# The largest routed expert moved ahead of the first pair of small experts in a two-layer denoising step

## The chip, the core and the metric

The kernel is one program on one core of a Trainium2 chip. The core has TensorE (PE in the profile, with its weight loads as PEld), VectorE (DVE), ScalarE (ACT), GpSimd (POOL) and SyncE (SP), which here issues nearly all transfers from HBM. The metric is the device time of one execution in microseconds (us); lower is better. The profile is one execution of its own.

## What is computed

The reference is a two-layer step over 128 context tokens and 128 latent tokens of width 1024, all in float32. Each layer has a mixer (attention in layer 0, a gated DeltaNet in layer 1) and then a mixture of 16 SwiGLU experts of inner width 512. Only the mixture matters here:

```python
in_group = (jnp.arange(N_EXPERTS) // EXPERTS_PER_GROUP)[None, :] == group_sel[:, None]
_, idx = lax.top_k(jnp.where(in_group, biased, -jnp.inf), TOP_K)
...
for e in range(N_EXPERTS):
    he = jax.nn.silu(x @ wg[e]) * (x @ wu[e])
    y = y + gates[:, e:e + 1] * (he @ wd[e])
```

Each of the 256 tokens goes to 2 of the 16 experts. The weights of an expert are three pieces of 2 MB: two halves of gate and up together (m = 0 and 1, each half of the contraction), and the down matrix (m = 2). So a layer reads 48 pieces of 2048 KB.

## The kernel before

**The ring.** All big weights of the program stream through `ring`, six slots of 2048 KB in SBUF, in one fixed order of positions. SyncE walks through that order: for each position it waits until the slot is free (`slot_free`, L1886) and issues one transfer (L1887). In a layer's expert stage the 48 positions are listed by `SEQ` (L43). In this text T0 to T47 are those 48 transfers. T(n) goes into the slot that T(n-6) held, so it can be issued when the last use of T(n-6) is over.

**Ranks and units.** Experts 4 and 5 of the model always come first, as ranks 0 and 1 (the fixed pair). The other 14 are sorted by their token count on the chip; rank 2 is the largest, rank 15 the smallest. `UNITS` (L42) gives the order in which ranks are worked on. A unit of two ranks is a pair: two experts with at most 32 tokens each, which share one block of 64 tokens. A unit of one rank is an expert with a block of 64 tokens of its own, or, for ranks 2, 3 and 4, two blocks of 64 one after the other on the same weights (`LEAN_CAP`, 128 tokens). `LEAN` lists the 14 blocks of a layer. (`FULL` is a second branch for token counts that do not fit; the profiled execution takes `LEAN`.) Within a pair `SEQ` alternates the two ranks: m = 0 of both, m = 1 of both, m = 2 of both.

**A block on TensorE.** `products` (gate and up, L544), `combined` of the block before (L570), two pairs of transposes (L475 and L587), then `down` (L562). Between them ScalarE and VectorE make SiLU(gate) * up, and GpSimd has gathered the block's tokens ahead of it (L885). The slots are given back by the last block that uses them: m = 0 in the middle of `products` by TensorE itself (L547), m = 1 after `products`, when ScalarE has read the result (L650), m = 2 after `down` (L658):

```python
for r in freed(plan, n):
    act.sem_inc(slot_free[slot_of(n0, r, m)], 1)
```

`freed(plan, n)` (L450) names the ranks that no later block uses. So the first of the two blocks of rank 2, 3 or 4 gives back nothing, and the second gives back three slots.

**The start of a stage.** T0 to T5, the fixed pair, are loaded before the stage starts. The fixed pair's `products` run ahead of the routing's end; ScalarE then gives back four slots at once (T6 to T9 are issued), and its `down`, much later, the other two (T10 and T11).

Of the kernel before, what the change touches and what calls it, by code (L numbers as in the profile page):

```python
# [38 lines left out]

FIXED = (4, 5)  # L40
FIXED_CAP, FIXED_SLOTS = 32, 64
UNITS = ((0, 1), (8, 9), (2,), (5,), (10, 11), (3,), (6,), (12, 13), (4,), (7,), (14, 15))  # L42
SEQ = [(r, m) for unit in UNITS for m in range(3) for r in unit]  # L43
LEAN_CAP = (FIXED_CAP,) * 2 + (128,) * 3 + (64,) * 3 + (32,) * 8


def full_cap(r):

    return T if r < 2 else min(T, 2 * T // (r - 1))


LEAN = [b for unit in UNITS for b in ([tuple((r, 0) for r in unit)] if len(unit) == 2 else
                                      [((unit[0], 64 * j),) for j in range(LEAN_CAP[unit[0]] // 64)])]
FULL = LEAN[:1] + [((r, at),) for unit in UNITS for r in unit for at in range(FIXED_CAP if r < 2 else 0, full_cap(r), 64)]
SLOTS_PAD = 3 * T
# [1977 lines left out]
```

## Time and profile before

| what | value |
|---|---|
| median of 3 runs | 1121.9 us (1112.18 to 1123.24) |
| profiled execution, its own time | 1118.37 us |
| its span, first to last instruction | 1116.4 us |
| PE busy | 980.3 us (88% of the span) |
| ring<-slots transfers | 138 of 2048 KB each |
| DMA over the span | 268 GB/s on average |
| granted TensorE clock, mean | 0.934 |

Of the page's 40 slices, those from about 280 us to 515 us and from about 880 us to 1088 us are the two expert stages; there the line with GB/s shows 424 to 430 in most slices. PE's share of the span is an average over stages that have different limits, and a slow or waiting PE can look busy. Times inside a stage are given in us from the span's start.

### The profile page before, as it was taken

To read this page: it belongs to the slowest core of one execution; us is meant where nothing else is said; L and a number is where in the kernel's file an instruction comes from. 1 tells how busy PE (TensorE), PEld (TensorE's weight loads), DVE (VectorE), ACT (ScalarE), POOL (GpSimd) and SP (SyncE) were. 2 spreads that over 40 slices of the span, in tenths; PEclk is the share of its full clock that TensorE was granted. 3 is DMA by queue.
4 is the path that set the end of the run, shared out by engine and by line. 5 is a ranking of instruction groups with operands and counts; after the bars stand their busy time and mean duration, and the time that the engine had idled before them with its cause. 6 is when DMAs were issued, how large, how long until landed. Compare 5 with 4: busy or idle time off the path is not lost. (4 is left out here: it accounts for less than half of the span.)

```text
span 1116.4 us, 13823 instructions
## 1 busy us (share of the span) xinstructions
PE 980.3 (88%) x5476; PEld 568.5 (51%) x5476; DVE 346.9 (31%) x816; ACT 216.9 (19%) x513; POOL 134.5 (12%) x149
## 2 busy tenths in 40 slices
PE   4799999797889898987999999888696989898996
PEld 1344456675333342336787668678584423333334
DVE  0100115238201000024333676668516400101014
ACT  1211045112200010003233421213103210000013
POOL 1000000001000000001000166566001000000000
PEclk8699998896989999998999899989897889999999
DMA  9985782053899999996564500222225499999991
GB/s 382 424 354 217 291 333 93 1 213 166 331 430 428 424 429 428 426 427 293 198 254 161 216 2 1 76 76 76 76 83 219 189 415 427 427 429 426 429 420 42
DMA packets 22444, 299.50 MB, mean 268 GB/s; under 512 B 2592, under 2 KB 2720, under 8 KB 4320
## 3 DMA queue, kind: packets, MB, share of 16 engines
q1 hardware_dynamic: 20880, 292.45, 64.0%
q0 software_dynamic: 1488, 6.03, 1.4%
q8 instruction: 49, 0.80, 0.3%
q14 instruction: 27, 0.22, 0.1%
HBM read 295.32 MB, written 3.15 MB: 267 GB/s over the span
## 5 line engine op out<-in xcount | busy, mean ns | idle before, releaser
L544 PE MATMUL bank<-ring,arena 128*32 128x512 f32 (+1 forms) x1216 | 203.6, 610 | 6.5 <-DMA ring<-slots 6.5
L562 PE MATMUL bank<-ring,arena 128*32 128x512 f32 (+1 forms) x608 | 111.7, 665 | 30.9 <-DMA ring<-slots 25.8
L544 PEld LDWEIGHTS bank<-ring,arena 128*32 128x32 f32 (+1 forms) x1216 | 61.3, 125 | 144.3 <-issue 133.6
L818 DVE TENSOR_TENSOR arena<-arena,bank 128x256 f32<-128x256 f32 x28 | 11.8, 421 | 301.5 <-ACT arena L647 301.5
L972 PE MATMUL bank<-act_t,ring 128*128 128x256 f32 x384 | 89.2, 386 | 6.3 <-DVE act_t L429 6.3
L1533 PE MATMUL bank<-ring,act_t 128*128 128x512 f32 x192 | 88.2, 615 | 3.9 <-ACTq L279 3.9
L972 PEld LDWEIGHTS bank<-act_t,ring 128*128 128x128 f32 x384 | 72.2, 193 | 20.0 <-DVE act_t L429 6.7
L562 PEld LDWEIGHTS bank<-ring,arena 128*32 128x32 f32 (+1 forms) x608 | 31.5, 133 | 92.6 <-issue 82.7
L307 PE MATMUL bank<-ring,par 128*32 128x512 f32 x384 | 54.6, 693 | 15.2 <-DMA ring<-slots 14.0
L885 POOL COPY arena<-arena 128x512 f32 (+1 forms) x34 | 17.5, 515 | 393.1 <-PE bank L544 306.7
L902 PE MATMUL bank<-act_t,ring 128*128 128x256 f32 x256 | 61.2, 402 | 1.6 <-ACT act_t L1264 0.9
L1533 PEld LDWEIGHTS bank<-ring,act_t 128*128 128x128 f32 x192 | 36.7, 196 | 50.7 <-issue 46.8
L570 PE MATMUL bank<-arena 64*128 64x256 f32 x448 | 55.9, 389 | 1.7 <-ACTq L467 1.7
L902 PEld LDWEIGHTS bank<-act_t,ring 128*128 128x128 f32 x256 | 51.9, 204 | 10.3 <-ACT act_t L1264 1.2
L570 PEld LDWEIGHTS bank<-arena 64*128 64x128 f32 x448 | 41.0, 186 | 28.6 <-issue 21.3
L647 ACT ACTIVATE arena<-bank 128x256 f32<-128x256 f32 x28 | 10.7, 383 | 180.2 <-PE bank L544 180.2
L659 ACT ACTIVATE arena<-bank 128x512 f32<-128x512 f32 x28 | 16.7, 597 | 141.3 <-PE bank L562 141.3
L441 POOL TENSOR_SCALAR res<-res,small 128x256 f32<-128x256 f32 x24 | 12.9, 550 | 239.9 <-DVE act_t L429 239.9
L326 DVE TENSOR_TENSOR mod<-bank,par 128x8 f32<-128x8 f32 x24 | 3.8, 161 | 115.0 <-PE bank L319 115.0
L319 PEld LDWEIGHTS bank<-par,o_delta 128*128 128x128 f32 x192 | 26.5, 212 | 15.8 <-ACT o_delta L313 11.7
L822 DVE COPY arena<-bank 128x256 f32<-128x256 f32 x28 | 11.9, 425 | 67.1 <-PE bank L587 67.1
L307 PEld LDWEIGHTS bank<-ring,par 128*32 128x32 f32 x384 | 11.3, 119 | 40.3 <-issue 39.5
(320 smaller groups left out, 1290.4 us busy)
## 6 DMA issues: line engine op xcount, KB each, us to landing
ring<-slots SPq DMA_DIRECT2D x138, 2048.0 KB, 12.5
cst<-consts SPq DMA_DIRECT2D x1, 1260.5 KB, 31.8
act_t<-x_t POOLq DMA_DIRECT2D x1, 1024.0 KB, 12.4
ring<-state POOLq DMA_DIRECT2D x1, 1024.0 KB, 7.7
out_st<-arena POOLq DMA_DIRECT2D x4, 256.0 KB, 2.8
out_y<-arena SPq DMA_DIRECT2D x4, 256.0 KB, 2.1
par<-params SPq DMA_DIRECT2D x1, 613.0 KB, 4.0
arena<-nat_bias POOLq DMA_DIRECT2D x1, 512.0 KB, 20.2
```

The source lines that it names most:

```text
L307: last = pe.matmul(bk[32 * j:32 * j + 32, :], p_("cond")[:, 32 * c:32 * c + 32], w[:, c, :], start=(c < 4), stop=(c >= 4))
L319: last = pe.matmul(bk[:, 2 * m:2 * m + 2], ada_rowbuf[:, job % 2, m * P:(m + 1) * P], p_("fold")[:, 0:2], start=True, stop=True)
L441: pool.tensor_scalar(res[:, c, :], res[:, c, :], ln_scaled[:, 0 + i:i + 1], ln_scaled[:, 64 + i:65 + i], ALU.mult, ALU.add).then_inc(S("re ...
L544: last = pe.matmul(bk[to:to + wide, :], x[:, 4 * m + c, wide * e:wide * e + wide], w[:, c, 512 * t:512 * t + 512], start=(m == 0 and c == ...
L562: last = pe.matmul(bank[3][to:to + wide, :], ht[:, col + wide * e:col + wide * e + wide], w[:, f, 512 * t:512 * t + 512], start=(f == 0), ...
L570: last = pe.matmul(bank[4 + d // 2][:, (d % 2) * T:(d % 2) * T + T], yb[64 * t:64 * t + 64, b, o * P:(o + 1) * P], gb[64 * t:64 * t + 64, ...
L659: act.activation(yb[:, n % 2, :], bank[3][:, :], ACT.Copy).then_inc(S("y_copied"), 1)
L822: dve.tensor_copy(gb[:, n % 2, :], bank[n % 2][:, 0:256]).then_inc(S("gates_moved"), 1)
L885: last = pool.tensor_copy(xe[:, n % 2, :, wide * e:wide * e + wide], xg[:, :, bass.ds(at + j, wide)])
L902: last = pe.matmul(out_bank(q, b, o), w[:, c, m * P:(m + 1) * P], act_t[:, c, :], start=(c == 0), stop=(c == KC - 1))
L972: last = pe.matmul(bank[i % 3][:, 0:T], w[:, c, (i % 4) * P:(i % 4 + 1) * P], act_t[:, c, :], start=(c == 0), stop=(c == KC - 1))
L1533: last = pe.matmul(bank[n % 4][:, :], act_t[:, c, s * P:(s + 1) * P], w[:, c, :], start=(c == 0), stop=(c == KC - 1))
```

## The change

```diff
-UNITS = ((0, 1), (8, 9), (2,), (5,), (10, 11), (3,), (6,), (12, 13), (4,), (7,), (14, 15))
+UNITS = ((0, 1), (2,), (8, 9), (5,), (10, 11), (3,), (6,), (12, 13), (4,), (7,), (14, 15))
 SEQ = [(r, m) for unit in UNITS for m in range(3) for r in unit]
```

Rank 2, with its two blocks, now stands directly behind the fixed pair, and the pair of ranks 8 and 9 behind it. `SEQ`, `LEAN` and `FULL` follow from the table, and so the order of transfers, of TensorE's blocks and of the gathers, in both layers. SyncE's instructions are the same as before, wait for wait; only the weights that a transfer fetches differ. T6 to T11 were ranks 8 and 9 and T12 to T14 were rank 2; now T6 to T8 are rank 2 and T9 to T14 are ranks 8 and 9.

On TensorE, in the LEAN branch of layer 0, directly behind the fixed pair's `down` (64x512 is a block of one expert, 32x512 that of a pair), there stood before:

```order
L544 MATMUL bank<-ring,arena 32x512 x32
L570 MATMUL bank<-arena 128x256 x8
L475 MATMUL bank<-cst,arena 128x128 x2
L587 MATMUL bank<-cst,arena 128x128 x2
L562 MATMUL bank<-ring,arena 32x512 x16
L544 MATMUL bank<-ring,arena 64x512 x16
```

In the same place there stands now:

```order
L544 MATMUL bank<-ring,arena 64x512 x16
L570 MATMUL bank<-arena 128x256 x8
L475 MATMUL bank<-cst,arena 128x128 x2
L587 MATMUL bank<-cst,arena 128x128 x2
L562 MATMUL bank<-ring,arena 64x512 x8
L544 MATMUL bank<-ring,arena 64x512 x16
```

The pair's block is gone from there, and the two blocks of rank 2 follow each other. On TensorE two blocks further on, directly ahead of rank 5, there stood before the second block of rank 2:

```order
L544 MATMUL bank<-ring,arena 64x512 x16
L570 MATMUL bank<-arena 128x256 x8
L475 MATMUL bank<-cst,arena 128x128 x2
L587 MATMUL bank<-cst,arena 128x128 x2
L562 MATMUL bank<-ring,arena 64x512 x8
L544 MATMUL bank<-ring,arena 64x512 x16
```

And now the pair of ranks 8 and 9:

```order
L544 MATMUL bank<-ring,arena 32x512 x32
L570 MATMUL bank<-arena 128x256 x8
L475 MATMUL bank<-cst,arena 128x128 x2
L587 MATMUL bank<-cst,arena 128x128 x2
L562 MATMUL bank<-ring,arena 32x512 x16
L544 MATMUL bank<-ring,arena 64x512 x16
```

The last row of each is rank 5, which stands where it stood. Layer 1 changes in the same way.

## Rows read from the trace of the kernel before

**Rows 1.** Busy time by stretch, inside both expert stages.

```profile
core 0: us, PE busy (x) PEld busy (x) DVE busy (x) ACT busy (x) POOL busy (x), PEclk, DMA share, GB/s
315.00:320.00 5.00, 3.01 (x16) 0.91 (x20) 0.00 (x0) 0.00 (x0) 0.00 (x0) 0.50 1.02 434
...
310.00:515.00 205.00, 177.63 (x1060) 72.37 (x1060) 28.99 (x80) 24.61 (x53) 7.32 (x14) 0.97 1.01 428
907.00:1085.00 178.00, 163.64 (x962) 62.43 (x960) 17.43 (x54) 16.08 (x37) 7.16 (x14) 0.96 1.01 428
```

**Rows 2.** TensorE's timeline, layer 0: start, us, line, count, [idle before, releaser].

```profile
302.95 7.05 PE L544 MATMUL bank<-ring,arena 128*32 128x512 f32 x64
...
316.99 5.71 PE L562 MATMUL bank<-ring,arena 128*32 128x512 f32 x32 [4.48 <-DMA ring<-slots]
...
326.69 3.65 PE L544 MATMUL bank<-ring,arena 128*64 128x512 f32 x16 [0.41 <-DMA ring<-slots]
...
336.60 7.04 PE L544 MATMUL bank<-ring,arena 128*64 128x512 f32 x32
...
349.89 7.04 PE L544 MATMUL bank<-ring,arena 128*64 128x512 f32 x32
...
493.66 3.64 PE L562 MATMUL bank<-ring,arena 128*32 128x512 f32 x32 [2.88 <-DMA ring<-slots]
```

**Rows 3.** TensorE's waits in layer 0, one releaser: us in total, times, longest.

```profile
PE bank L562 <- DMA ring<-slots: 13.5, 4, 4.5
```

**Rows 4.** L1887, layer 0, one transfer at a time: issue (T10, T18, T47), landing.

```profile
L1887 SPq DMA_DIRECT2D ring<-slots x1: 338/338/338, 303.4 to 303.4; - x1
...
DMA to landing us min/median/max: 7.9/7.9/7.9
...
L1887 SPq DMA_DIRECT2D ring<-slots x1: 338/338/338, 340.4 to 340.4; - x1
...
DMA to landing us min/median/max: 11.2/11.2/11.2
...
L1887 SPq DMA_DIRECT2D ring<-slots x1: 338/338/338, 481.5 to 481.5; - x1
...
DMA to landing us min/median/max: 12.0/12.0/12.0
```

**Rows 5.** SyncE's issues in layer 0: start, us (T12, T19, T20).

```profile
306.76 0.34 SPq L1887 DMA_DIRECT2D ring<-slots  x1
...
343.88 0.34 SPq L1887 DMA_DIRECT2D ring<-slots  x1
...
350.30 0.34 SPq L1887 DMA_DIRECT2D ring<-slots  x1
```

**Rows 6.** A transfer issued alone, long before the stage (L1887).

```profile
L1887 SPq DMA_DIRECT2D ring<-slots x1: 328/328/328, 177.9 to 177.9; - x1
...
DMA to landing us min/median/max: 7.5/7.5/7.5
```

**Rows 7.** Layer 1: transfers T10 and T18, issue and landing (L1887).

```profile
L1887 SPq DMA_DIRECT2D ring<-slots x1: 338/338/338, 899.9 to 899.9; - x1
...
DMA to landing us min/median/max: 7.8/7.8/7.8
...
L1887 SPq DMA_DIRECT2D ring<-slots x1: 338/338/338, 937.4 to 937.4; - x1
...
DMA to landing us min/median/max: 10.8/10.8/10.8
```

**Rows 8.** TensorE's timeline, layer 1.

```profile
899.47 7.17 PE L544 MATMUL bank<-ring,arena 128*32 128x512 f32 x64
...
912.79 6.47 PE L562 MATMUL bank<-ring,arena 128*32 128x512 f32 x32 [3.63 <-DMA ring<-slots]
...
923.73 3.65 PE L544 MATMUL bank<-ring,arena 128*64 128x512 f32 x16 [0.89 <-DMA ring<-slots]
...
1090.25 3.64 PE L562 MATMUL bank<-ring,arena 128*32 128x512 f32 x32 [2.83 <-DMA ring<-slots]
```

## The prediction

> **What bounds the kernel now.** First the page's slices, to find the two expert stages, since the change touches nothing else. Then the busy time by stretch inside them: in both the DMA engines are busy throughout (share 1.01 in each long stretch) at 428 GB/s [rows 1]. TensorE is busy for 177.63 of 205 us in the first, so it looks nearly as loaded; but the waits say who waits for whom. In layer 0 TensorE waits for weights in `down` four times, 13.5 us in all [rows 3], once for each pair behind the fixed one, the last time in front of the very last piece (at 493.66 [rows 2]); nothing in the stretch shows the transfers short of free slots for long enough to stop. So the stage ends when its 48th piece has landed, plus one `down`; what TensorE does earlier decides only when slots come free.
>
> The pace of the stream: T18 is issued at 340.4 and lands 11.2 us later, at 351.6; T47 is issued at 481.5 and lands at 493.5 [rows 4]. 29 pieces in 141.9 us is **4.89 us a piece**. Layer 1 runs alike: T18 lands at 937.4 + 10.8 = 948.2 [rows 7], the last wait ends at 1090.25 [rows 8], 4.90 us a piece. A unit's price on TensorE is about the same for every block, 13.29 us from one block's start to the next (336.60 to 349.89 [rows 2]), but its price in pieces is not: a pair takes 6 pieces, 29.3 us of stream, a one-block expert 14.7 us, and rank 2, 3 or 4 takes 14.7 us of stream for 26.6 us of TensorE, and holds its slots through most of them.
>
> **The change part by part.** No instruction is added or removed. GpSimd makes one gather less ahead of the first block behind the fixed pair and one more two blocks later; TensorE comes to these blocks 13 us apart, which hides a gather, and VectorE's and ScalarE's work only changes places. Their cost is nothing, and if the cover were gone it would be one gather. SyncE's queue has the same waits in the same order, so what counts is when each wait is met. I follow the slots through layer 0.
>
> T6 to T9 are issued when the fixed pair's `products` are over, T10 and T11 when its `down` is over (303.4 [rows 4]); neither depends on who comes next. T10 lands at 311.3, T11 4.89 us later at 316.2.
>
> Before, the block behind the fixed pair was ranks 8 and 9, started at 302.95 [rows 2]. It uses its slots once, so 3.81 us after its start SyncE could already issue T12 (306.76 [rows 5]), five more followed, and the stream never ran dry.
>
> Now rank 2 starts there at the same 302.95 (its pieces are T6 to T8; the pair in this place began on T6 to T9 and did not wait). Its first block gives back nothing. The second starts 13.29 us later, at 316.24. From rank 2's second block before, which started at 336.60 [rows 2], the offsets of its releases can be read: T18 was issued 3.80 [rows 4], T19 7.28 and T20 13.70 us after it [rows 5]. So now **T12 is issued at 320.04, T13 at 323.5, T14 at 329.9**. At 320.04 nothing is left in flight, since T11 landed at 316.2. How long a piece takes into an empty stream is bounded by the nearest rows: 7.5 us [rows 6] for one issued quite alone, 7.9 and 7.8 us for T10 [rows 4, 7], which others follow closely. T12 here is alone for 3.5 us; I take the middle, 7.75, so it lands at 327.8. Without the hole it would have landed at 316.2 + 4.89 = 321.1; the hole is 6.7 us.
>
> Behind T12 the stream holds. T13 could land at 331.3 by its issue and at 332.7 by the pace, so the pace decides; T14 comes out level (337.7 by issue, 337.6 by pace). Ranks 8 and 9 start at 316.24 + 13.29 = 329.5 and give back their first halves 3.81 us later, so T15 and T16 are issued from 333.3 on, ahead of the 334.8 at which T15 is due at that lead of 7.75 us (342.5 by pace); T17 and T18 follow on the second halves, about 337 to 338. So T18 lands at 327.8 + 6 x 4.89 = 357.1, against 351.6 before: **5.5 us late**. Before was not at the ideal pace in this stretch: from T10 at 311.3 to T18 at 351.6 it took 40.3 us for 8 pieces, 5.04 each. If the six pieces behind the hole run at that, T18 lands at 358.0, 6.4 us late. I take 5.9, since the irregular pieces before lay among issues in quick succession and half of that remains.
>
> The Trainium skill has a fit for one transfer ("DMA: Bandwidth & Descriptors", section Anatomy of one DMA: about 2.0 us and the bytes at 436 GB/s), made on another issuing path than SyncE's. By it a lone piece of 2.1 MB would take an estimated 6.8 us and the sum would be 1.9 us smaller over both layers; the rows show 7.5 and more, so the rows are used.
>
> Layer 1 has the same steps: 899.47 [rows 8] + 13.29 + 3.80 = 916.56 for T12, landing at 924.3, and T18 at 953.7, against 948.2: 5.5 us late; at the pace that stretch had (907.7 to 948.2, 8 pieces, 5.06 each) it is 6.5. I take 5.9 again.
>
> Is the delay kept? From T18 on the order of units is the old one. TensorE is now short of weights: rank 5 starts at 329.5 + 13.3 = 342.8, waits a little for T16 (347.4) and is done near 357; the pair 10, 11 waits for T19 (362.0), T21 (371.8) and T23 (381.6) and is over 3.6 us behind the last, at 385, or at 389 if that `down` runs at half the clock. Rank 3's first block starts behind T24 (386.5) or at 389, its second 13.3 us later, at 400 to 402, and releases T30 at 404 to 406, which could land at 413.7 at the latest and is due by pace at 357.1 + 12 x 4.89 = 415.8. So there is no second hole, with 2 us to spare, and from there on the old picture comes back, shifted. The next stage's weights go into slots that the last pair gives back, so they shift too, and the work between the two expert stages hangs on the first one's end. What TensorE no longer waits for in ranks 8, 9 and 2 (4.48 and 0.41 us in layer 0 [rows 2]) it waits for later, in ranks 5, 10 and 11.
>
> The sum is 5.9 + 5.9 = 11.8 us (10.9 to 12.9 by the bounds). On the profiled execution's 1118.37 us (span 1116.4) that is 1130.2 us; on the median of the runs shown, 3.5 us above it, 1133.7. I take **1133 us**, about 1% more.
>
> **The rivals.** *TensorE's lost time comes back.* The change puts 26.6 us of TensorE's work over 14.7 us of stream just where TensorE stood still for weights. If TensorE set the stage's end, layer 0 would gain the 4.48 and 0.41 us of waiting and the 2.07 us by which the `down` behind the wait ran long (5.71 against 3.64 [rows 2]; the granted clock there is 0.50, the lower of its two levels, behind the 4.48 us of idle time [rows 1]), and layer 1 3.63 + 0.89 + 2.83 [rows 8]: 14.3 us, 1104 us on the profile and 1107.6 on the median. For it speaks that PE is busy in 87% of the stretch; against it that every later pair waits for its last piece again [rows 3] and the last one up to the end.
>
> This rival is what the Trainium skill would make one expect: "Perfetto Trace Analysis", section Optimization Strategies under DMA, sets as the goal to keep the matmul engine as highly used as possible. The stretch's own rows contradict it here, since the stream is full and TensorE's use can rise only by taking slots from it.
>
> *Only one of the two holes counts.* If the work between the stages were waiting for something that does not hang on the first stage, or if pieces behind a hole came faster than 4.89 us, one hole's 5.9 us would vanish: 1124.3 on the profile, 1127.8 on the median, no change within what can be told. The rows show the stream at a steady 428 GB/s with all engines busy, so it cannot catch up inside a stage; the chain between stages I have no row against.
>
> *A second hole at rank 3.* The pair 10, 11 now waits three times for 3.6 to 6.3 us. After 4.48 us of waiting the trace shows a `down` that begins at the lower clock. If more of the pair's halves and of rank 3's first block run so, at 3.5 us more for each, the 2 us to spare are gone and up to 3.5 us a layer come on top: 1137 on the profile, 1140.7 on the median. It decides when rank 3's second block starts later than 404 in the changed trace's layer 0.
>
> **How the numbers follow.** Forecast 0.76, one hole only 0.10, TensorE's time 0.05, second hole 0.09. About 1% is what a measurement of this kernel can tell from no change, here 11.2 us, just under the forecast's 11.8; so of the forecast's 0.76 I put 0.50 above the line and 0.26 inside it. That gives slower 0.59, same 0.36, faster 0.05. The range: the forecast by its bounds is 1129 to 1135, the runs before lay up to 10 us below their median and 1.3 above, and it should take in part of the two nearest rivals: 1123 to 1139. It leaves out the fast rival and the far ends of the other two, about 0.15.
>
> **What would show it.** In the changed trace T12 is issued 16.6 us behind T10 instead of 3.4, and lands 11 to 12 us behind T11; the DMA share drops below 1 for some 6 us near 316 to 322 and near 913 to 919 and nowhere else in the stages; ranks 8 and 9 run without a wait; the pair 10, 11 waits at both halves; the last `down` of layer 0 waits until about 499.5, that of layer 1 until about 1102. If T12 is issued at 306, or the stream still runs dry nowhere, the forecast is wrong; if layer 0 ends 6 us late and layer 1's start is not, the second rival is right.

## The result and the profile after

Four runs of the changed kernel have a median of 1136.15 us (1132.28 to 1141.19); before, on the same occasion, 1122.57 us (1112.18 to 1123.87). The ratio is 1.0158, 95% interval 1.0119 to 1.0197: **slower by 1.6%**. The 1133 us on record are inside what was measured, but stand for a change of 1.0%, on the border of what can be told; the size was too small. On the 1121.9 us that the forecast started from, the measured ratio gives 1139.6 us, 0.6 us above the upper end of its range.

The profiled execution after is the longest of the four: 1141.19 us, span 1139.3, against 1118.37 and 1116.4. So its 22.9 us over before must first be divided. I cut each span at T6's issue and T47's landing of both stages:

| piece of the span | before | after | difference |
|---|---|---|---|
| up to T6's issue, layer 0 | 281.9 | 287.7 | 5.8 |
| stage of layer 0 (T6's issue to T47's landing) | 211.6 | 220.1 | 8.5 |
| from there to T6's issue, layer 1 | 385.6 | 387.1 | 1.5 |
| stage of layer 1 | 211.0 | 218.2 | 7.2 |
| the rest | 26.3 | 26.2 | -0.1 |

15.6 us lie in the two stages. Whether the 5.8 us ahead of them belong to the change is a question for the experiments.

The busy time by stretch after, layer 0, in the form of [rows 1]:

```profile
310.00:320.00 10.00, 9.74 (x56) 4.10 (x52) 1.36 (x4) 0.77 (x2) 0.80 (x2) 1.00 0.96 395
320.00:327.00 7.00, 7.00 (x34) 2.31 (x32) 0.00 (x0) 0.60 (x1) 0.00 (x0) 1.00 0.17 43
327.00:515.00 188.00, 162.72 (x996) 62.71 (x994) 17.30 (x54) 16.36 (x36) 6.70 (x13) 0.95 1.00 424
```

There is the hole: 7 us in which the DMA engines move 43 GB/s instead of 428, while TensorE is busy for all 7.00 of them at full clock. Single transfers of layer 0 after (L1887; T10, T12 and T14, each issue with its time to landing) answer to [rows 4]:

```profile
L1887 SPq DMA_DIRECT2D ring<-slots x1: 337/337/337, 308.8 to 308.8; - x1
...
DMA to landing us min/median/max: 7.7/7.7/7.7
...
L1887 SPq DMA_DIRECT2D ring<-slots x1: 342/342/342, 325.7 to 325.7; - x1
...
DMA to landing us min/median/max: 8.5/8.5/8.5
...
L1887 SPq DMA_DIRECT2D ring<-slots x1: 338/338/338, 335.6 to 335.6; - x1
...
DMA to landing us min/median/max: 9.4/9.4/9.4
```

T12 is issued nearly 17 us behind T10 (before 3.4), and T14 nearly 27 us behind it. TensorE's timeline of the same stretch, in the form of [rows 2]:

```profile
308.51 7.09 PE L544 MATMUL bank<-ring,arena 128*64 128x512 f32 x32
...
321.85 7.04 PE L544 MATMUL bank<-ring,arena 128*64 128x512 f32 x32
...
335.24 7.07 PE L544 MATMUL bank<-ring,arena 128*32 128x512 f32 x64
...
345.12 3.64 PE L562 MATMUL bank<-ring,arena 128*32 128x512 f32 x32 [0.29 <-ACT arena L655]
350.00 3.65 PE L544 MATMUL bank<-ring,arena 128*64 128x512 f32 x16 [1.24 <-DMA ring<-slots]
354.80 3.66 PE L544 MATMUL bank<-ring,arena 128*64 128x512 f32 x16 [1.15 <-DMA ring<-slots]
...
369.58 6.05 PE L544 MATMUL bank<-ring,arena 128*32 128x512 f32 x32 [4.70 <-DMA ring<-slots]
379.50 6.21 PE L544 MATMUL bank<-ring,arena 128*32 128x512 f32 x32 [3.87 <-DMA ring<-slots]
...
408.89 7.04 PE L544 MATMUL bank<-ring,arena 128*64 128x512 f32 x32
...
507.90 5.16 PE L562 MATMUL bank<-ring,arena 128*32 128x512 f32 x32 [3.34 <-DMA ring<-slots]
```

Rank 2's two blocks start at 308.51 and 321.85, 13.34 us apart, and ranks 8 and 9 at 335.24 run through without waiting for weights (345.12 waits only for ScalarE). The waits come back at rank 5, 1.24 and 1.15 us, and at the pair 10, 11, 4.70 and 3.87 us in front of its two halves. TensorE's waits for weights in layer 0, from the fixed pair's `down` to the end of the stage, sum to 22.1 us now:

```profile
PE bank L544 <- DMA ring<-slots: 14.2, 7, 4.7
PE bank L562 <- DMA ring<-slots: 7.9, 3, 3.5
```

Before, they summed to 17.3 us, the 13.5 us in `down` [rows 3] and these in `products`:

```profile
PE bank L544 <- DMA ring<-slots: 3.8, 4, 1.3
```

In `down` they fell from 13.5 us to 7.9, and in `products` they rose from 3.8 to 14.2. A reader who looked only at the first number would think the change had worked.

### The profile page after: what moved, and what is told of

The parts are those of the page before. It is cut to its first block and busy times, and to the rows that moved or that the text cites. A ratio compares the mean times of both kernels' runs of the same rounds, so it can differ in the third digit from the quotient of the medians.

```text
span 1139.3 us, 13823 instructions
## 1 busy us (share of the span) xinstructions
PE 991.2 (87%) x5476; PEld 573.9 (50%) x5476; DVE 347.1 (30%) x816; ACT 216.8 (19%) x513; POOL 134.4 (12%) x149
## 5 line engine op out<-in xcount | busy, mean ns | idle before, releaser
L544 PE MATMUL bank<-ring,arena 128*32 128x512 f32 (+1 forms) x1216 | 211.8, 639 | 27.6 <-DMA ring<-slots 27.6
L562 PE MATMUL bank<-ring,arena 128*32 128x512 f32 (+1 forms) x608 | 108.3, 641 | 21.7 <-DMA ring<-slots 16.0
L818 DVE TENSOR_TENSOR arena<-arena,bank 128x256 f32<-128x256 f32 x28 | 11.8, 421 | 317.0 <-ACT arena L647 317.0
L972 PEld LDWEIGHTS bank<-act_t,ring 128*128 128x128 f32 x384 | 72.2, 193 | 19.9 <-DVE act_t L429 6.7
L307 PE MATMUL bank<-ring,par 128*32 128x512 f32 x384 | 55.5, 703 | 15.7 <-DMA ring<-slots 14.6
L902 PEld LDWEIGHTS bank<-act_t,ring 128*128 128x128 f32 x256 | 51.6, 202 | 10.1 <-ACT act_t L1264 1.2
L647 ACT ACTIVATE arena<-bank 128x256 f32<-128x256 f32 x28 | 10.7, 383 | 210.4 <-PE bank L544 210.4
```

The lines of the kernel that those rows point to most:

```text
L307: last = pe.matmul(bk[32 * j:32 * j + 32, :], p_("cond")[:, 32 * c:32 * c + 32], w[:, c, :], start=(c < 4), stop=(c >= 4))
L544: last = pe.matmul(bk[to:to + wide, :], x[:, 4 * m + c, wide * e:wide * e + wide], w[:, c, 512 * t:512 * t + 512], start=(m == 0 and c == ...
L562: last = pe.matmul(bank[3][to:to + wide, :], ht[:, col + wide * e:col + wide * e + wide], w[:, f, 512 * t:512 * t + 512], start=(f == 0), ...
L902: last = pe.matmul(out_bank(q, b, o), w[:, c, m * P:(m + 1) * P], act_t[:, c, :], start=(c == 0), stop=(c == KC - 1))
L972: last = pe.matmul(bank[i % 3][:, 0:T], w[:, c, (i % 4) * P:(i % 4 + 1) * P], act_t[:, c, :], start=(c == 0), stop=(c == KC - 1))
```

## The experiments

The theory, from here on the hole theory: a stage is as long as its stream of 48 pieces; rank 2 holds three of six slots through two blocks, and with rank 2 first there is nothing else to give back, so the stream stands still once in every stage. The rivals: a loss outside the stages; a loss from the order of the pieces itself; TensorE's time deciding; and, within the theory, which slot sets the hole. The table has the stage lengths of each run's profiled execution (T6's issue to T47's landing, us) and the ratio to before of the timed runs. Edits of `UNITS` are shown against the kernel before, the others against the changed kernel; before_early_down and after_early_down are one edit on either.

| kernel | layer 0 | layer 1 | ratio, 95% interval |
|---|---|---|---|
| before | 211.6 | 211.0 | |
| after | 220.1 | 218.2 | 1.0158 (1.0119 to 1.0197) |
| only_l0: new order in layer 0 alone | 219.6 | 212.3 | 1.0086 (1.0053 to 1.0119) |
| only_l1: new order in layer 1 alone | 212.6 | 219.0 | 1.0073 (1.0038 to 1.0108) |
| one_block_first: rank 5 in rank 2's place | 211.5 | 211.3 | 0.9982 (0.9941 to 1.0022) |
| two_doubles: ranks 2 and 3 in front | 232.6 | 230.8 | 1.0345 (1.0262 to 1.0429) |
| after_gates_first | 219.4 | 219.2 | 1.0117 (1.0061 to 1.0173) |
| after_no_second | 211.7 | 211.0 | 1.0010 (0.9978 to 1.0043) |
| before_early_down | 214.9 | 216.6 | 1.0054 (1.0020 to 1.0088) |
| after_early_down | 229.0 | 228.8 | one execution only, 1160.49 us |
| after_again | 219.8 | 218.5 | 1.0135 (1.0093 to 1.0176) |

**One layer at a time.** `UNITS` becomes one table for each layer, and `SEQ`, `LEAN` and `FULL` with it:

```diff
-UNITS = ((0, 1), (8, 9), (2,), ...
-SEQ = [(r, m) for unit in UNITS for m in range(3) for r in unit]
+UNITS = (
+    ((0, 1), (2,), (8, 9), (5,), (10, 11), (3,), (6,), (12, 13), (4,), (7,), (14, 15)),
+    ((0, 1), (8, 9), (2,), (5,), (10, 11), (3,), (6,), (12, 13), (4,), (7,), (14, 15)))
+SEQ = [[(r, m) for unit in units for m in range(3) for r in unit] for units in UNITS]
```

Layer 0 alone (only_l0):

> The new order in layer 0 alone, the old one in layer 1. Hole theory: each stage pays by itself, because SyncE's stream stands still from T11's landing until rank 2's second block gives back T12's slot. Then layer 0's stage, from T6's issue to T47's landing, takes 219 to 221 us (before 211.7, after 220.1) and layer 1's 210.5 to 212 (before 211.0, after 218.2): about 8 us over before, ratio 1.005 to 1.009. Rival, one cause outside the stages (start of the program or the way between the stages): the stages' lengths do not follow the order layer by layer, and the ratio is either near 1.00 or near the full 1.016.

And with the two tables exchanged (only_l1):

> The old order in layer 0, the new one in layer 1. Hole theory: layer 0's stage 211 to 213 us, layer 1's 217 to 219, ratio 1.005 to 1.008, and the excess of this run and of the run with the new order in layer 0 alone add up to the full change. Rival, one hole only counts: this run or the other one shows nothing at the program's end although its stage is longer.

Measured: the stage with the new order is 219.6 and 219.0 us, the one with the old order 212.3 and 212.6. Each kernel pays about half: 0.86% and 0.73%, together the 1.6% of the full change. So the loss sits in the stages, each pays by itself, and each counts at the end; that the first stage's delay would vanish on the way is refuted.

**Another expert in the same place** (one_block_first), with one block:

```diff
-UNITS = ((0, 1), (8, 9), (2,), (5,), (10, 11), ...
+UNITS = ((0, 1), (5,), (8, 9), (2,), (10, 11), ...
```

> Rank 5, an expert of one block, directly behind the fixed pair in both layers; then ranks 8 and 9, then rank 2. Hole theory: what costs is not a single expert in this place but two blocks on the same slots. Rank 5 gives back its first slot 3.8 us after its start, T12 is issued about 3.4 us behind T10 as before, no hole, stages of 211 to 213 us, ratio 0.997 to 1.003. Rival, any expert of three pieces ahead of the pair starves the stream (three pieces for 13.3 us of TensorE instead of six): stages of 215 us or more, ratio 1.007 or more. Rival, TensorE's time decides: it no longer waits behind the fixed pair, ratio below 0.995.

Measured: 0.998, stages of 211.5 and 211.3 us. It is not an expert ahead of the pair that costs. TensorE no longer waits directly behind the fixed pair, but its waits for weights have only moved: in layer 0 they sum to 18.8 us, against 17.3 before. So this run says nothing against the rival that TensorE's time decides. T12 of layer 0, issued 3.5 us behind T10 (at 307.0), finds the stream full, so it lands only after 14.8 us:

```profile
L1887 SPq DMA_DIRECT2D ring<-slots x1: 341/341/341, 310.5 to 310.5; - x1
...
DMA to landing us min/median/max: 14.8/14.8/14.8
```

**The suspect doubled** (two_doubles):

```diff
-UNITS = ((0, 1), (8, 9), (2,), (5,), (10, 11), (3,), (6,), ...
+UNITS = ((0, 1), (2,), (3,), (8, 9), (5,), (10, 11), (6,), ...
```

> Ranks 2 and 3, both of two blocks, directly behind the fixed pair in both layers. Hole theory: a second hole opens, since T15 waits for rank 3's second block, which starts three blocks of 13.29 us behind the first: issue about 27 us behind T12 and an extra 11 to 13 us of standing still, so stages of 230 to 233 us (the after kernel 220 and 218) and 1155 to 1164 us, ratio 1.032 to 1.038. Rival, the loss comes once, from moving the pair away from the fixed pair: stages as after, ratio 1.012 to 1.02. Rival, TensorE's time decides: ratio at or below the after kernel's.

Measured: ratio 1.0345 and stages of 232.6 and 230.8, some 12.5 us more than after. The second hole is where it was expected. T14 of layer 0 is issued at 333.0 and lands 9.6 us later, at 342.6; T15 waits for rank 3's second block and lands at 357.4, 14.8 us behind T14:

```profile
L1887 SPq DMA_DIRECT2D ring<-slots x1: 338/338/338, 333.0 to 333.0; - x1
...
DMA to landing us min/median/max: 9.6/9.6/9.6
...
L1887 SPq DMA_DIRECT2D ring<-slots x1: 338/338/338, 349.7 to 349.7; - x1
...
DMA to landing us min/median/max: 7.7/7.7/7.7
```

**The second block taken away** (after_no_second). The transfers stay; rank 2's second block is left out, so some of its tokens get no output from it:

```diff
-    [((unit[0], 64 * j),) for j in range(LEAN_CAP[unit[0]] // 64)])]
+    [((unit[0], 64 * j),) for j in range(1 if unit[0] == 2 else LEAN_CAP[unit[0]] // 64)])]
```

> The order of after, but rank 2's second block is left out (those of its tokens that stand in the second block get no output from it), with the same transfers and releases one block earlier. Hole theory: the second block's 13.3 us on the same slots are the whole loss, so without it no hole, stages of 211 to 213 us, ratio 0.995 to 1.003: taking 13.3 us of TensorE's work out of each stage wins about 7.5, and nothing against before. Rival, TensorE's time decides: about 13.3 us a stage less than after, ratio about 0.99. Rival, the order of the transfers itself costs (rank 2's pieces ahead of the pair's): stages stay at 217 to 220.

Measured: 211.7 and 211.0, ratio 1.001. Without that block, in the new order of pieces, the loss is gone. And 13.3 us of TensorE's work less in each stage brings nothing below before: TensorE's time does not decide.

**Which slot.** In after_gates_first TensorE runs both `products` of rank 2 before both `down`, and ScalarE's reads follow:

```diff
                 for n in range(1, len(plan)):
+                    if plan is LEAN and n == 2:
+                        continue
                     pe.wait_ge(S("xe_ready"), block_count(L, n))
                     products(plan, n)
                     combined(plan, n - 1)
+                    if plan is LEAN and n == 1:
+                        pe.wait_ge(S("xe_ready"), block_count(L, 2))
+                        products(plan, 2)
+                        outputs(plan, 1)
+                        combined(plan, 1)
+                        outputs(plan, 2)
+                        continue
                     outputs(plan, n)
```

> The order of after, but TensorE runs gate and up of both blocks of rank 2 first and the two down steps behind them, so the first two slots of rank 2 come back about 4.5 and 1 us earlier and the third (down) at the same time as in after. What binds, T12 or T14? If T12's slot sets the loss (the forecast's reading, with T14 only level), T12 lands 4 to 4.5 us earlier against T10's issue and so does everything behind it: stages of 214 to 216 us, ratio about 1.007. If T14's slot, rank 2's down weights that are held to the end of the second block, sets it, the hole only moves from T12 to T14: T14 lands 35 to 36 us behind T10's issue as in after (36.1 and 35.5), stages of 218 to 220, ratio 1.011 to 1.018.

Measured: T10 of layer 0 is issued at 300.0, T12 at 312.5 and T14 at 327.7 (the line of the issue is L1901 here).

```profile
L1901 SPq DMA_DIRECT2D ring<-slots x1: 342/342/342, 312.5 to 312.5; - x1
...
DMA to landing us min/median/max: 8.1/8.1/8.1
...
L1901 SPq DMA_DIRECT2D ring<-slots x1: 338/338/338, 327.7 to 327.7; - x1
...
DMA to landing us min/median/max: 9.0/9.0/9.0
```

T12 lands 20.6 us behind T10's issue, almost 5 us earlier than after (25.4), and T14 36.6 us behind it, as in after (36.1). The stages are 219.4 and 219.2: nothing is won. T12's slot comes back some 4.3 us sooner behind T10 than after, T14's 0.9 us later. So T14's slot, that of rank 2's down weights, holds the loss up by itself when T12's comes back sooner; the forecast had T14 only level with the pace. What T12's slot alone would cost, with T14's free in time, no run shows.

**The fixed pair's `down` earlier** (before_early_down, and the same edit on after), ahead of the gathering of the other tokens on TensorE, and ScalarE's part in the same way:

```diff
                 if plan is LEAN:
+                    outputs(plan, 0)
                     rest_of_slots(xg_base)
-                outputs(plan, 0)
+                else:
+                    outputs(plan, 0)
```

> The order of before, with the fixed pair's down step ahead of the gathering of the other experts' tokens, so T10 and T11 are issued some 13 us earlier. Theory that the stage is as long as its stream: T10 and T11 land at the pace, without the 0.5 to 1.7 us that T10 and T11 lose now; stages 0.5 to 2 us shorter, 209.5 to 211 us, ratio 0.996 to 1.000, within what can be told. Rival, TensorE's wait in this place is late for everybody: stages longer.

> The order of after, with the same earlier down step of the fixed pair. Hole theory: T10 and T11 land earlier, but T12's and T14's issue hangs on TensorE's two blocks of rank 2 and not on the stream, so the hole grows by what is won and stages stay at 218 to 220 us from T6's issue (T12 lands 14 us or more behind T11). Rival, the hole is a length of its own: stages shorter by the same 0.5 to 2 us as in the order of before.

Both expectations were wrong. T10 and T11 are issued early as meant, but the block behind comes later; TensorE's timeline of before_early_down, and the busy time of the stretch with the fixed pair's `down`:

```profile
280.08 0.69 PE L475 MATMUL bank<-cst,arena 128*128 128x128 f32 x2 [3.41 <-DVE arena L820]
...
281.24 1.93 PE L562 MATMUL bank<-ring,arena 128*32 128x512 f32 x8
284.37 5.18 PE L562 MATMUL bank<-ring,arena 128*32 128x512 f32 x24 [1.19 <-issue]
289.48 14.00 PE L523 MATMUL bank<-arena 128*128 128x512 f32 x32
306.04 8.77 PE L544 MATMUL bank<-ring,arena 128*32 128x512 f32 x64 [2.56 <-issue]
```

```profile
281.00:289.00 8.00, 6.76 (x33) 1.55 (x32) 1.31 (x5) 0.19 (x1) 0.00 (x0) 0.50 1.00 423
```

The same `down` in the kernel before:

```profile
299.49 3.64 PE L562 MATMUL bank<-ring,arena 128*32 128x512 f32 x32 [0.25 <-ACT arena L655]
```

TensorE now waits 3.41 us for VectorE, and behind that idle time the granted clock is 0.50, the lower of its two levels: the fixed pair's `down` takes 8.3 us (281.24 to 289.55) instead of 3.64. Ranks 8 and 9 start at 306.04, 29.1 us behind T6's issue (276.95) instead of 21.1, and their `products` take 8.77 us instead of 7.05. T12 follows at 311.57, 1.5 us after T11 has landed (310.11), and lands 10.1 us behind T11 instead of 4.9: a hole in a new place. The stages are 3.3 and 5.6 us longer than before. In the order of after the same edit makes the stages 8.9 and 10.6 us longer, where I had expected them unchanged: T12 lands 21.9 us behind T11 there. I had counted the pieces that would come sooner and not the slot that would come later, which is the hole theory's own rule. The runs agree with the theory, though not with what I made of it; the edit is no gain.

**The changed kernel again** (after_again, no edit):

> The after kernel itself once more, with more runs, since its profiled execution was 22.9 us longer in span than that of before and only 15.6 of these lie in the two stages (5.8 lie ahead of the first one). If the change is the holes alone, the stages are again 218 to 220.5 us and the ratio comes out at 1.012 to 1.015 (7 to 8.5 us in each stage on 1119 us). If the change also lengthens what lies ahead of the first stage, T6 is issued at 287 us or later again (before 281.9) and the ratio stays at 1.018 or more.

Measured: 1135.89 us against 1122.24, ratio 1.0135; stages of 219.8 and 218.5; T6 is issued at 279.9 us, earlier than before's 281.9. So the 5.8 us ahead of the first stage were that execution's and not the change's. Over the eleven profiled executions T6 of layer 0 is issued between 277.0 and 287.7 us, in no order that follows the edits.

## Why the prediction was right in kind and too small

**The bound and the mechanism** held. The stage ends with its stream, as before [rows 1]; T12 is issued 16.8 us behind T10 in after, after_again and the new-order layers of the one-layer kernels (16.65 worked out), nothing else is in flight then, and the stream stands still in the stretch named. Ranks 8 and 9 run without a wait, and the pair 10, 11 waits at both halves. T11 landed at 316.85 in the kernel before and not at the 316.2 worked out, which makes that hole 0.7 us shorter than the 6.7 us but does not enter the sum. Most of this is in the lines of the result, and the run without the second block takes the cause away, the one with two such experts adds a second and longer hole.

**The step that failed is the size of the hole: "T14 comes out level (337.7 by issue, 337.6 by pace)"**, and with it the 5.9 us a stage. The times to landing behind it were read from a piece alone, 7.75 us. T12, which is alone, took 7.7 to 8.5 us in the three executions with the new order in layer 0 and the three with it in layer 1, 8.0 on average. T14 is issued 2.7 to 3.5 us before T13 lands, and took 9.4, 9.6, 10.2 in layer 0 and 8.8, 8.7, 9.5 in layer 1, 9.4 on average. So T14 lands 1.6 us later than by the 7.75, and the stream continues from its landing: T18 comes 19.5 to 19.9 us behind it, four pieces at the pace. So these 1.6 us count almost in full. T12 adds some 0.4 us (issued 0.2 us later than worked out, and 8.0 us to landing instead of 7.75). The 0.4 us a stage that the forecast had put on top, for pieces that come irregularly among quick issues, covers a part of this by luck: T13 and the pieces behind T14 come at the pace, and T14 alone is late. Measured: with the new order 219.8 on average in layer 0 and 218.6 in layer 1 (after, after_again and the one-layer kernels), with the old 212.1 and 211.7 (before and the one-layer kernels): **7.7 and 6.9 us a stage, 14.6 together, against 11.8**. That is 1.3% of 1119 us, inside the intervals of both timings of the change (1.0119 to 1.0197 and 1.0093 to 1.0176). The rest of the first timing's 1.58% is within its interval and not explained by anything in the stages.

In the stream this is a short second gap at T14. Two windows of 1 us of after, layer 0, ahead of T13's landing at 339.1:

```profile
337.00:338.00 1.00, 1.00 (x16) 0.37 (x12) 0.00 (x0) 0.00 (x0) 0.00 (x0) 1.00 0.95 262
338.00:339.00 1.00, 1.00 (x16) 0.26 (x8) 0.00 (x0) 0.00 (x0) 0.00 (x0) 1.00 0.77 311
```

Two microseconds at 262 and 311 GB/s, against 442 and 426 in the windows to either side, are an estimated 0.7 us of lost pace, in the middle of a stretch that the forecast took as full; T14 lands 5.9 us behind T13 here, 1.0 us over the pace. Why T14 takes longer than a piece issued alone is not settled: T10, also issued while one piece is under way, took 7.7 us in layer 0 of after and 9.2 in layer 1. That stays open.

**The kept delay** held: the holes are not caught up inside a stage, and the first one's reaches the end (only_l0).

**The rivals.** TensorE's time: refuted by after_no_second. One hole only: refuted by only_l0 and only_l1. A second hole at rank 3: it does not appear. The pair's two halves did run long (6.05 and 6.21 us, where both halves of ranks 8 and 9 together took 7.07), as the rival wanted, and rank 3's second block started at 408.89, that is 403.4 on the time scale of the forecast, which is 5.45 us behind at T10; the point from which it would decide was 404. Yet the stream has no hole there: T30, whose issue that block sets, is issued 5.8 us before T29 lands, and lands 4.90 us behind it, at the pace. By the forecast's 7.75 us it could have landed 3.0 us before that.

The Trainium skill ("Perfetto Trace Analysis", section Optimization Strategies under DMA) sets as the goal to keep the matmul engine as highly used as possible. That would have led the wrong way here: in the seven microseconds of the hole TensorE is used to the full. The Trainium skill's fit for one transfer on GpSimd's path ("DMA: Bandwidth & Descriptors", section Anatomy of one DMA) gives an estimated 6.8 us for this size. The pieces read here that SyncE issued into an empty stream took longer, 7.5 to 9.0 us.

## What to carry to other kernels

Where a stage is bound by a stream through a ring of buffers, price each unit by how long it holds its buffers, not only by its compute and its bytes: put a unit that holds slots for twice its own load time only where the pieces behind it are already in the ring. Look at the slot that is given back last, since it can hold the loss up when the others come back sooner, and remember that an engine's wait that goes away in one place is paid where the stream is still full. An edit that frees buffers sooner is no gain if it makes the next release later.

## What was not expected of the hardware

A 2048 KB piece does not have one price. In a full stream each lands 4.89 us behind the one before; into an empty one it took 7.5 us [rows 6] to 9.0 (T14 of after_gates_first in layer 0; 7.6 in layer 1); and T14 of the new order, issued 2.7 to 3.5 us before the stream would run out, took 8.7 to 10.2. It landed 5.4 to 7.5 us behind T13, so the stream lost 0.5 to 2.6 us against its pace there although a piece was in flight throughout. And the time up to the first expert stage varies by 10.7 us (277.0 to 287.7) between profiled executions whose program is the same up to there, which is most of the scatter of what lies outside the two stages (688.0 to 701.0 us in the same executions). In before_early_down a wait of 3.41 us was followed by a `down` at half the granted clock that took 8.3 us instead of 3.64.
